# Two weight blocks of an MLP on one Trainium2 core: the second block's split moved into the second product, the first block's sums moved from GpSimd to VectorE

## The reference

```python
y_ctx, y_lat = token_mixer(hc, hx, p, rows, need_ctx)
x = x + mod[:, :, 2] * y_lat
x = x + mod[:, :, 5] * sq_relu_mlp(modulate(x, norm2_g[l], mod, 3), mlp_w1[l], mlp_w2[l])
# sq_relu_mlp(h, w1, w2) = jnp.square(jax.nn.relu(h @ w1)) @ w2
return rmsnorm(x, final_g)
```

## Time and profile before

| | before |
|---|---|
| median of 3 runs | 2979.53 us |
| profiled execution: device time / span | 2981.87 us / 2980.1 us |
| TensorE matmul busy | 2598.8 us, 87% |
| VectorE / ScalarE / GpSimd busy | 1678.6 / 1003.6 / 564.4 us |
| mean granted TensorE clock | 0.94 |
| projection and token split (1390.0 to 1600.6) | TensorE busy 184.14 of 210.60 us |
| U(0), U(1), D(0) of pass 0 (1600.6 to 1678.0) | TensorE busy 64.03 of 77.40 us |
| U(2) to U(15) of pass 0 (1678.0 to 2300.3) | TensorE busy 552.36 of 622.30 us |
| pass 1 from its D(0) on (2380.9 to 2966.2) | TensorE busy 585.30 of 585.30 us |

### The profile page before, as it was taken

One profiled execution on the slowest core, in us unless ns is written; L12 is line 12 of the kernel. 1 busy time (PEld: TensorE's weight loads), 2 busy tenths in 40 slices (PEclk: granted clock), 3 DMA queues, 4 the chain that ended last, 5 costly groups with the idle time before them and its releaser, 6 DMA issues.

```text
span 2980.1 us, 37444 instructions
## 1 busy us (share of the span) xinstructions
PE 2598.8 (87%) x14900; PEld 1405.8 (47%) x14900; DVE 1678.6 (56%) x2786; ACT 1003.6 (34%) x1919; POOL 564.4 (19%) x406
## 2 busy tenths in 40 slices
PE   7789989673888989976995898898988999999998
PEld 2344564231585859664452343343433444444443
DVE  5752444676675756446347666666665544444445
ACT  2743443653142423222455322323323311122222
POOL 0400000000928261012135322323221000000000
PEclk9899999886899999998997899999999999999999
...
GB/s 200 103 40 39 32 59 14 0 15 21 75 22 93 24 75 14 16 44 134 1 120 110 144 68 134 104 98 134 72 129 100 232 78 78 78 75 61 62 76 71
DMA packets 121621, 226.99 MB, mean 76 GB/s; under 512 B 14280, under 2 KB 59848, under 8 KB 116968
## 3 DMA queue, kind: packets, MB, share of 16 engines
...
## 4 chain that ended last, share of the span: by engine, by line
PE 50%; issue 17%; DVE 12%; POOL 10%; ACT 8%; DMA 3%; SPq 0%; POOLq 0%; DVEq 0%; ACTq 0%
PE pb L2100 19%; PE pb L2080 14%; PE pb L286 7%; DVE arena L1625 5%; POOL arena L1155 2%; ACT arena L1089 2%; POOL arena L1158 2%; PE pb L2039 2%; POOL arena L1161 1%; ACT arena L1106 1%; POOL MS L1172 1%; DMA w2x<-arena 1%; PE pb L1727 1%; DVE arena L1675 1%; DMA arena<-in_ada_rest 1%
## 5 line engine op out<-in xcount | busy, mean ns | idle before, releaser
L2100 PE MATMUL pb<-arena 128*128 128x512 f16 x3072 | 699.9, 390 | 80.9 <-DVE arena L1700 80.9
L2080 PE MATMUL pb<-arena 128*128 128x512 f16 x2688 | 589.7, 381 | 19.0 <-issue 14.0
L2100 PEld LDWEIGHTS pb<-arena 128*128 128x128 f16 x3072 | 306.6, 100 | 469.3 <-DVE arena L1700 88.8
L1700 DVE SCALAR_TENSOR_TENSOR arena<-pb,arena 128x512 f32<-128x512 f32 x512 | 349.6, 690 | 208.3 <-PE pb L2100 207.7
L286 PE MATMUL pb<-arena 128*128 128x512 f16 (+1 forms) x1992 | 425.1, 375 | 21.9 <-ACT arena L960 10.2
L2080 PEld LDWEIGHTS pb<-arena 128*128 128x128 f16 x2688 | 263.8, 98 | 340.1 <-issue 20.1
L1675 DVE TENSOR_TENSOR arena<-arena,pb 128x512 f32<-128x512 f32 x224 | 149.3, 685 | 295.2 <-PE pb L2080 294.4
L286 PEld LDWEIGHTS pb<-arena 128*128 128x128 f16 x1992 | 195.4, 99 | 248.9 <-issue 20.3
L1625 DVE SCALAR_TENSOR_TENSOR arena<-arena 128x512 f16<-128x512 f32 (+1 forms) x144 | 190.5, 1352 | 91.7 <-ACT arena L1047 80.4
L1089 ACT ACTIVATE arena<-pb 128x512 f32<-128x512 f32 x32 | 19.1, 597 | 636.8 <-PE pb L2080 628.8
L1089 ACT ACTIVATE arena<-arena 128x512 f32<-128x512 f32 x256 | 160.5, 627 | 170.9 <-DVE arena L1675 166.8
...
## 6 DMA issues: line engine op xcount, KB each, us to landing
...
arena<-in_x SPq DMA_DIRECT2D x128, 128.0 KB, 4.2
...
```

Of the source, the lines that this page charges most:

```text
L1700: dve.scalar_tensor_tensor(xs, pb[:, 4 + n % 4, :], 1.0 / (WS * AS), xs, ALU.mult, ALU.add).then_inc(S("acc"), 1)
L2080: mm = pe.matmul(pb[:, (7 * g + j) % 4, :], W1P[sl][WDEST[a]][0][:, ws, P * k:P * k + P], token_op(b, L // 2, slice(0, BLK))[:, k, hs, :], ...
L2100: mm = pe.matmul(pb[:, 4 + n % 4, :], ACTP[sl][:, 2 * f + th, hs, P * tt:P * tt + P], W2P[sl][:, f, ws, BLK * dh:BLK * dh + BLK], start=(f ...
```

## The change

1. **Second weights' lo parts.** The two lo parts of task (2, s) leave the end of U(s) on VectorE. They now come after n = 10 and n = 13 of D(s-1); those of (2, 0) come after U(0).
2. **First weights' sums.** `w_add` moves from GpSimd to VectorE. Sums 1 to 3 of (1, s+3) come after n = 15 of D(s); sum 4 comes behind the second lo part of the task. GpSimd keeps only the gates.
3. **Ahead of the first pass.** The token splits start one step earlier in the loop, the loop is shorter, and what is left is done in a list `LAST_SPLITS`: three of the last pair's token splits, then five of (1, 0)'s, and the other six mixed. U(0) no longer waits for all token splits at once but, at each product, for the one that it reads.
4. **`final_g` and the output.** The row is loaded right after the second weight task, into another place, and there are four output buffers in place of three.
5. Three semaphores of the convolutions become one, with the same waits.

VectorE in one U and D of pass 0, the kernel before: L1675 are the adds, L1625 the lo parts of weights, L1700 the accumulations, L1660 the activations' lo parts.

```diff
@@ -447,7 +447,7 @@
         for w, x in TASKS:
-            ADDS.append(ADDS[-1] + (4 if w == 1 else 2))
+            ADDS.append(ADDS[-1] + (0 if w == 1 else 2))
             SPLITS.append(SPLITS[-1] + (7 if w == 1 else 2))
@@ -473,8 +473,10 @@
-            mid = [(TASK[1, s + 1], i) for i in range(1, 8)] if s < NSET - 1 else []
-            return mid + [(TASK[2, s], i) for i in range(1, 3)]
+            return [(TASK[1, s + 1], i) for i in range(1, 8)] if s < NSET - 1 else []
+
+        LAST_SPLITS = [("o", 1), ("o", 2), ("o", 3)] + [("w", i) for i in range(1, 6)] + [("o", 4), ("w", 6), ("w", 7),
+                                                                                         ("o", 5), ("o", 6), ("o", 7)]
@@ -494,8 +496,8 @@
-        fgbc = view(206, [D])
-        outb = [view(at, [D]) for at in (64, 68, 210)]
+        fgbc = view(200, [D])
+        outb = [view(at, [D]) for at in (64, 68, 206, 210)]
         junk_f = m5bc
@@ -694,6 +696,8 @@
             load_task(1)
+            sp.wait_ge(S("h_sq"), N5 + NT)
+            sp.dma_start(fgbc, dr["final_g"].broadcast_to([P, D])).then_inc(S("row_in"), 16)
             for k in range(2, len(TASKS)):
@@ -705,12 +709,11 @@
             fetch(2, 0)
-            sp.dma_start(fgbc, dr["final_g"].broadcast_to([P, D])).then_inc(S("row_in"), 16)
...
                     sp.wait_ge(S("z_out"), z + 1)
-                    store_tokens(sp, ORD[8 * (1 - pas) + z % 8], outb[z % 3], S(f"out_st{z % 3}"))
+                    store_tokens(sp, ORD[8 * (1 - pas) + z % 8], outb[z % 4], S(f"out_st{z % 4}"))
@@ -1048,7 +1051,7 @@
                 op = WSEQ[i - 1]
-                act.wait_ge(S("g_add"), ADDS[k] + (1, 1, 2, 2, 3, 4, 4)[i - 1])
+                act.wait_ge(S("w_sum"), 4 * x + (1, 1, 2, 2, 3, 4, 4)[i - 1])
                 if i in (4, 6):
@@ -1063,7 +1066,7 @@
-            for t in range(NT + 4):
+            for t in range(NT + 2):
                 if t < NT:
@@ -1078,12 +1081,11 @@
                     ins.then_inc(S("h_aff"), 1)
-                if t >= 4:
-                    for i in range(1, 5) if t % 2 == 0 else range(5, 8):
-                        o_hi((t - 4) // 2, i)
-                if t in (14, 15):
-                    for i in range(1, 6) if t == 14 else range(6, 8):
-                        w_hi(0, i)
+                if t >= 3 and t < NT + 1:
+                    for i in range(1, 5) if t % 2 else range(5, 8):
+                        o_hi((t - 3) // 2, i)
+            for kind, i in LAST_SPLITS:
+                o_hi(NT // 2 - 1, i) if kind == "o" else w_hi(0, i)
@@ -1095,7 +1097,7 @@
                 work = work_up(s) if pas == 0 else []
-                for x in work[:7 if s < NSET - 1 else 0]:
+                for x in work:
                     w_hi(*x)
@@ -1104,8 +1106,9 @@
                     act.activation(ACTP[s % 2][:, b, 0, :], CB4[b], ACT.Copy).then_inc(S("s_hi"), 1)
-                for x in work[7 if s < NSET - 1 else 0:]:
-                    w_hi(*x)
+                if pas == 0:
+                    for i in range(1, 3):
+                        w_hi(TASK[2, s], i)
@@ -1183,28 +1186,6 @@
-            def w_add(k, parts):
...
@@ -1221,16 +1202,13 @@
-            for t in range(NT + 3):
-                if t < NT:
-                    pool.wait_ge(S("h_ms"), N5 + t + 1)
-                    pool.tensor_tensor(rst2[:, t:t + 1], ssq2[:, t:t + 1], mhalf[:], ALU.pow).then_inc(S("h_rs"), 1)
-                if t >= 3 and t % 2:
-                    o_add((t - 3) // 2, (1, 2, 3))
-                if t >= 4 and t % 2 == 0:
-                    o_add((t - 4) // 2, (4,))
-                if t in (13, 14):
-                    w_add(0, (1, 2, 3) if t == 13 else (4,))
+            for t in range(NT):
+                pool.wait_ge(S("h_ms"), N5 + t + 1)
+                pool.tensor_tensor(rst2[:, t:t + 1], ssq2[:, t:t + 1], mhalf[:], ALU.pow).then_inc(S("h_rs"), 1)
+                if t >= 2:
+                    o_add((t - 2) // 2, (4,) if t % 2 else (1, 2, 3))
+            o_add(NT // 2 - 1, (1, 2, 3))
+            o_add(NT // 2 - 1, (4,))
@@ -1241,8 +1219,6 @@
             for s in range(NSET):
-                if s < NSET - 1:
-                    w_add(TASK[1, s + 1], (1, 2, 3, 4))
                 w_gate(TASK[2, s])
@@ -1412,8 +1388,8 @@
                 wc = col("rgc", 4 * j, 4)
-                conv(XR[:, 0:L], 4, wc, ZR).then_inc(S("rg_cv"), 1)
-                conv(XR[:, L:LT], 4, wc, ZC, n=TC).then_inc(S("rg_cv"), 1)
+                conv(XR[:, 0:L], 4, wc, ZR).then_inc(S("cv"), 1)
+                conv(XR[:, L:LT], 4, wc, ZC, n=TC).then_inc(S("cv"), 1)
                 split_lo(dve, jx["i"] + 2)
@@ -1614,6 +1590,28 @@
+            def w_add(k, parts):
+                x = TASKS[k][1]
+                p0, p1, p2, p3 = w1_blocks(k)
+                q, r = w1_source(k, 5), w1_source(k, 4)
+                a = 4 * x
+                if 1 in parts:
+                    dve.wait_ge(S(f"stage_in{k % 2}"), 32 + 16 * (k // 2 + 1 + 3 * ((k + 1) % 2)))
+                    if x == 1:
+                        dve.wait_ge(S("g_lo"), 7)
+                    if x >= 2:
+                        dve.wait_ge(S("u_mm"), 7 * (x - 1))
+                        dve.wait_ge(S(f"gw1{x % 2}"), 16 * (x // 2))
+                    dve.tensor_tensor(q, p0, p3, ALU.subtract).then_inc(S("w_sum"), 1)
+                    dve.wait_ge(S("w_sum"), a + 1)
+                    dve.tensor_tensor(p3, p3, p2, ALU.add).then_inc(S("w_sum"), 1)
+                    dve.wait_ge(S("w_sum"), a + 2)
+                    dve.tensor_tensor(r, p3, p0, ALU.subtract).then_inc(S("w_sum"), 1)
+                if 4 in parts:
+                    dve.wait_ge(S("w_sum"), a + 3)
+                    dve.wait_ge(S("g_lo"), SPLITS[k] + 2)
+                    dve.tensor_tensor(p1, p1, r, ALU.subtract).then_inc(S("w_sum"), 1)
+
             def w_lo(k, i):
@@ -1623,6 +1621,8 @@
                 dve.scalar_tensor_tensor(lo, src, WS, hi, ALU.mult, ALU.subtract).then_inc(S("g_lo"), 1)
+                if w == 1 and i == 2:
+                    w_add(k, (4,))
@@ -1631,7 +1631,7 @@
             dve.wait_ge(S("x_in3"), TOK0 + 16 * CPT * EARLY)
-            for t in range(NT + 4):
+            for t in range(NT + 1):
                 if t < NT:
@@ -1647,12 +1647,12 @@
                     dve.tensor_scalar(xn2[u % 2], x1(u), rst2[:, u:u + 1], None, ALU.mult).then_inc(S("h_xn"), 1)
-                if t >= 4:
-                    for i in range(1, 5) if t % 2 == 0 else range(5, 8):
-                        o_lo((t - 4) // 2, i)
-                if t in (14, 15):
-                    for i in range(1, 6) if t == 14 else range(6, 8):
-                        w_lo(0, i)
+                if t >= 3:
+                    for i in range(1, 5) if t % 2 else range(5, 8):
+                        o_lo((t - 3) // 2, i)
+            w_add(0, (1, 2, 3))
+            for kind, i in LAST_SPLITS:
+                o_lo(NT // 2 - 1, i) if kind == "o" else w_lo(0, i)
@@ -1662,7 +1662,7 @@
                 work = work_up(s) if pas == 0 else []
-                spread = [work[2 * m:2 * m + 2] for m in range(3)] + [work[6:7], work[7:]] if s < NSET - 1 else [[]] * 4 + [work]
+                spread = [work[2 * m:2 * m + 2] for m in range(4)]
                 bank = lambda j: pb[:, (7 * g + j) % 4, :]
@@ -1673,7 +1673,7 @@
                     dve.tensor_tensor(dst, src, bank(j), ALU.add).then_inc(S("u_c"), 1)
-                    for x in spread[{0: 0, 1: 1, 2: 2, 4: 3, 6: 4}[m]] if m in (0, 1, 2, 4, 6) else []:
+                    for x in spread[{0: 0, 1: 1, 2: 2, 4: 3}[m]] if m in (0, 1, 2, 4) else []:
                         w_lo(*x)
@@ -1684,9 +1684,9 @@
                         dve.wait_ge(S("row_in"), 48)
-                    if y >= 3:
-                        dve.wait_ge(S(f"out_st{y % 3}"), 16 * CPT * (y // 3))
-                    dve.scalar_tensor_tensor(outb[y % 3], o_tile(pas, y % 8), rst2[:, y:y + 1], fgbc, ALU.mult, ALU.mult
+                    if y >= 4:
+                        dve.wait_ge(S(f"out_st{y % 4}"), 16 * CPT * (y // 4))
+                    dve.scalar_tensor_tensor(outb[y % 4], o_tile(pas, y % 8), rst2[:, y:y + 1], fgbc, ALU.mult, ALU.mult
                                              ).then_inc(S("z_out"), 1)
@@ -1701,11 +1701,16 @@
                         a_lo(dg + 1, s + 1, n // 2 + 1)
+                    if pas == 0 and n == 15 and s + 3 < NSET:
+                        w_add(TASK[1, s + 3], (1, 2, 3))
+                    if not last and pas == 0 and n in (10, 13):
+                        w_lo(TASK[2, s + 1], n // 3 - 2)
                     if last and n in (7, 11, 15):
...
+            w_add(TASK[1, 1], (1, 2, 3))
             for pas in range(2):
@@ -1713,6 +1718,10 @@
                                 a_lo(NSET * pas, 0, i)
+                            if pas == 0:
+                                for i in range(1, 3):
+                                    w_lo(TASK[2, 0], i)
```

(4 more changed lines are left out.)

40 lines of the change are left out of this document (10 added, 30 removed).

## The result

The changed kernel takes 2862.48 us, the median of four runs (2858.05 to 2866.97); the kernel before, run beside it, 2978.57 (2977.22 to 2987.02). The ratio is 0.9605, with a 95% interval of 0.9579 to 0.963. The forecast was 2868, the range 2856 to 2893; the gain is 116 us by the medians, where 113 was forecast. The profiled execution took 2865.34 us.

The account below looks back on a forecast made before the run. TensorE bounds it, stopped in each D while VectorE is late by its order. Gains 99.1 (U(2) to U(15)) + 11 (start) + 0 + 3.1 (end of pass 0) = 113 us off 2981.87 give 2868 us, range 2856 to 2893.

Parts of the forecast that it names:

- The sum: Whole kernel: gains of 99.1, 11, 0 and 3.1 make 113 us, taken off the profiled 2981.87 us.
- Second weights' lo parts into D: U(2) to U(15), pass 0: moving them ends TensorE's stop in each D and the low clock behind it, gain 99.1 us.
- The layout of U: VectorE's work in one U, laid out instruction by instruction: the last two adds end 19.3 us into U.
- the reserve: Start of D: the first accumulation may be 3.5 us later before TensorE stops at four banks.
- The gate beside VectorE: In U, GpSimd's gate some 6 to 12 us in stretches about 2.5 VectorE instructions, 3.9 us, without stopping TensorE.
- The sums' price: First weights' sums on VectorE in D: 0.7 us each, after L1660's 0.68; highest case 2.24 each.
- Sums leave GpSimd: Moving the first weights' sums to VectorE stops sum 4 holding back the gate; no time by itself.
- Ahead of U(0): Start of pass 0: U(0)'s start unchanged (4 us earlier to 6 later); U(0), U(1), D(0) gain 11 us, between 4 and 15.
- D(0)'s stop and the low clock behind it: Start of pass 0: D(0) waits 2.5 us for VectorE (perhaps 0.5 to 4), and low clock adds 2.
- End of pass 0: D(14) and D(15): stops of 1.60 and 1.03 us, the latter behind final_out's wait for final_g, go; gain 3.1 us.
- Rival 1: Part of TensorE's stop in each D stays, VectorE being late: 47 us less gain, 2915 us; chance 0.15.
- Rival 3: VectorE waits for the first weights' load at D's end, stopping TensorE: slower than before, 3063 us for a 45 us load; chance 0.03.

Follow-up runs that it names:

- e1_lo_only: Kernel before with only the second weights' lo parts moved into D, GpSimd keeping the sums: 2873.47 us, ratio 0.9633.
- e6_pad8: Changed kernel with eight extra 128x512 VectorE operations behind the last add of each U of pass 0 from U(2) on: 2914.95 us, ratio 0.9776.
- e2_sums_no_lo: Changed kernel with the second weights' lo parts put back at the end of U, sums staying on VectorE: 2910.09 us, ratio 0.976.
- e3_old_lead: Changed kernel with the old order of splits ahead of U(0), which waits for all token splits at once: 2865.61 us, ratio 0.9607.
- e4_late_g: Changed kernel with the load of final_g put back behind the second weights' fetch for pass 1: 2870.76 us, ratio 0.9623.

## Why the prediction was right

- **The sum.** The gain came out at 116 us for 113, and the start of the pass is the term that was too low. The forecast of 2868 was 5.5 us above the measured 2862.48: some 3 us are that gain, and 2.3 come from taking it off the profiled execution (2981.87) and not off the median (2979.53).
- **Second weights' lo parts into D.** Right in mechanism and in size: 99.2 us for 99.1, and e1_lo_only shows that this part alone brings it. The layout of U ended at 19.3 us, the trace says 19.5; the reserve was put at 3.5 and is 3.2, with 3.0 to 3.3 by e6_pad8. The second lo part costs 1.22 us for 1.18 predicted, and the first accumulation starts behind the last adds as laid out.
- **The gate beside VectorE.** 4.1 us for each set, 3.9 predicted. It starts 5.6 us into U, just ahead of the 6 to 12 given, and falls on lo 1 and lo 2, at 2.67 us each for the 2.24 taken. Sum 4, up to 2.2 predicted, takes 0.69 in the steady sets, because the gate is over. The lo parts' longer time and the sum's shorter one about cancel: sum 4 ends 12.0 us into U, where the layout had 11.6.
- **The sums' price.** As taken from L1660, and the end at 2.24, kept in the range, didn't occur. The grouped lines of the changed kernel from U(2) to D(14) (busy us, mean ns, idle before), sum 1 and sum 4:

```profile
L1605 DVE TENSOR_TENSOR arena<-arena 128x512 f32<-128x512 f32 x13 | 8.9, 681 | 0.0
L1613 DVE TENSOR_TENSOR arena<-arena 128x512 f32<-128x512 f32 x13 | 9.0, 693 | 1.3
```

- **Sums leave GpSimd: no time by itself.** This step held only on top of part 1, and failed as a statement of its own: e2_sums_no_lo gained 71 us, 70.9 of them from U(2) to D(14). I had looked for what waits for GpSimd, and nothing on the chain does. But GpSimd made VectorE's lo parts longer, ScalarE's chain later by that, and the stop is the end of this chain. What an engine costs others beside it is not in the view of who waits for it.
- **Ahead of U(0).** The forecast of 0 for U(0)'s start came out at 0.1; e3_old_lead agrees that the order is worth nothing. The start to U(2) gave 14.9 us for 11, at the upper end of the 4 to 15. That gain comes with part 1, as e1_lo_only shows (62.68 us) and e2_sums_no_lo from the other side (76.7). The step in error is D(0)'s stop and the low clock behind it, put at 2.5 and 2: they were 0.28, and none. D(0) ran at the full clock, 5.34 and 15.71 us. U(1)'s wait was 1.83 for 1.6, and U(0)'s clock 3.0 for 2.9.
- **End of pass 0.** 3.1 as predicted, by its two stops. What I missed is why the early row is needed: left late it would cost not the 1.03 us of before but 6.9, as e4_late_g shows.
- **Rivals.** None came. Rival 1's price holds where it applies: in e6_pad8, stops of 2.65 us on average cost 45 us in place of its 47 for 2.0 and 1.65 of low clock each, since fewer of them bring the low clock. The 1.65 was read off one D of the kernel before; over its 13 the 72 matmuls took 17.80 us on average, 2.3 more than the 15.54 of full pace, about every second one 18.3 or more. That rival also counts five more instructions for VectorE in each set. They are four, the sums, since VectorE had the lo parts before. Rival 3's loads were in time: VectorE waited for one in U(0), 6.42 us before the first sum at 1609.36, which is behind U(1)'s wait of 1.83; in the steady sets it never did (0.0 us ahead of L1605).
